# A decoder step's feed-forward part: up sums kept in PSUM, low parts shared anew between VectorE and GpSimd

## What is computed

```python
def merge_and_ffn(x, conv_out, attn_out, w_out, ffn_norm_g, w_gate, w_up, w_down):
    mix = jnp.concatenate([conv_out, attn_out.astype(conv_out.dtype)], axis=-1)
    x = x + jnp.einsum('bte,ed->btd', mix, w_out)
    h = rms_norm(x, ffn_norm_g)
    f = jax.nn.silu(jnp.einsum('btd,df->btf', h, w_gate)) * jnp.einsum('btd,df->btf', h, w_up)
    return x + jnp.einsum('btf,fd->btd', f, w_down)
```

## Time and profile before

| | us |
|---|---|
| median of 3 runs | 1693.53 |
| lowest and highest | 1683.49, 1693.72 |
| the profiled execution | 1688.96 |
| its span, first to last instruction | 1687.1 |
| TensorE busy in it | 1505.7 |
| VectorE busy | 1245.7 |
| GpSimd busy | 836.0 |
| ScalarE busy | 671.4 |

### The profile page before, as it was taken

One profiled execution on the slowest core, in us unless ns is written; L12 is line 12 of the kernel. 1 busy time (PEld: TensorE's weight loads), 2 busy tenths in 40 slices (PEclk: granted clock), 3 DMA queues, 4 the chain that ended last, 5 costly groups with the idle time before them and its releaser, 6 DMA issues.

```text
span 1687.1 us, 30660 instructions
## 1 busy us (share of the span) xinstructions
PE 1505.7 (89%) x10233; PEld 1371.8 (81%) x10233; DVE 1245.7 (74%) x2159; ACT 671.4 (40%) x1267; POOL 836.0 (50%) x643
## 2 busy tenths in 40 slices
PE   5999988889968878999889898999778999999889
PEld 4998767548756776999888888888778888988889
DVE  7799979999769844545867767666888666677775
ACT  4100268655356544522433333333243333333332
POOL 4544111211468400141766656666577666666664
PEclk9999989999969988999989999999889999999999
...
DMA packets 97160, 134.89 MB, mean 80 GB/s; under 512 B 15185, under 2 KB 51281, under 8 KB 96943
## 3 DMA queue, kind: packets, MB, share of 16 engines
...
## 4 chain that ended last, share of the span: by engine, by line
PE 50%; DVE 23%; issue 13%; ACT 7%; POOL 3%; DMA 2%; DVEq 1%; ACTq 0%; SPq 0%; POOLq 0%
PE ps L1162 14%; PE ps L1164 13%; PE ps L1163 13%; DVE raw_up L2987 2%; DVE mcnt L2578 2%; DVE ff L3043 2%; ACT f_hi L2231 2%; PE ps L1481 2%; PE ps L1469 1%; POOL w_lo L1093 1%; DVE x L3056 1%; DVE w_raw L2994 1%; ACT w_hi L2196 1%; DVE f_t L3031 1%; ACT rl L1904 1%
## 5 line engine op out<-in xcount | busy, mean ns | idle before, releaser
L1162 PE MATMUL ps<-hi_t,w_hi 128*128 128x272 f32 (+4 forms) x1672 | 498.2, 298 | 4.5 <-issue 2.5
L1164 PE MATMUL ps<-hi_t,w_lo 128*128 128x272 f32 (+4 forms) x1672 | 496.6, 297 | 0.0
L1163 PE MATMUL ps<-lo_t,w_hi 128*128 128x272 f32 (+4 forms) x1672 | 496.5, 297 | 0.0
L1162 PEld LDWEIGHTS ps<-hi_t,w_hi 128*128 128x128 f32 (+1 forms) x1672 | 315.8, 189 | 6.1 <-issue 4.1
L1163 PEld LDWEIGHTS ps<-lo_t,w_hi 128*128 128x128 f32 (+1 forms) x1672 | 315.7, 189 | 0.7
L1164 PEld LDWEIGHTS ps<-hi_t,w_lo 128*128 128x128 f32 (+1 forms) x1672 | 315.4, 189 | 0.6
L1162 PE MATMUL ps<-f_hi,w_hi 128*128 128x272 f32 x704 | 220.8, 314 | 83.5 <-DVE x L3056 66.5
L1093 POOL TENSOR_TENSOR w_lo<-w_raw,w_hi 128x512 fp32r<-128x512 f32 x132 | 185.1, 1402 | 133.0 <-ACT w_hi L2189 133.0
L1093 POOL TENSOR_TENSOR w_lo<-raw_up,w_hi 128x512 fp32r<-128x512 f32 x132 | 181.6, 1376 | 122.9 <-ACT w_hi L2189 122.9
L1162 PEld LDWEIGHTS ps<-f_hi,w_hi 128*128 128x128 f32 x704 | 140.2, 199 | 101.5 <-DVE x L3056 77.7
L1164 PE MATMUL ps<-f_hi,w_lo 128*128 128x272 f32 x704 | 211.3, 300 | 0.0
...
## 6 DMA issues: line engine op xcount, KB each, us to landing
raw_up<-in_w_up SPq DMA_DIRECT2D x88, 256.0 KB, 2.8
w_raw<-in_w_gate SPq DMA_DIRECT2D x88, 256.0 KB, 3.0
w_f<-in_w_down SPq DMA_DIRECT2D x88, 256.0 KB, 2.8
...
```

What stands on the lines that cost most here:

```text
L1162: pe.matmul(out, a_hi, b_hi, start=first, stop=False)
L1163: pe.matmul(out, a_hi, b_lo, start=False, stop=False)
L1164: return pe.matmul(out, a_lo, b_hi, start=False, stop=last)
```

## The change

- The sums of up (blocks 21, 11, 22 and 12) are written to the bank that the last of their products used, and stay there. `multiply` reads its up operand from the bank and writes the product into the same bank; `f_high` and `f_low` read it there. The tile `ff` is gone. TensorE's product 13 (step 6 of up), which writes the bank of block 21, now waits for that block's low part of f.
- The low parts of the down weights move from GpSimd to VectorE. Their high parts stand at the head of ScalarE's pair (two) and behind operand 10 (two); in pair 0 they stand later.
- GpSimd's low parts of gate and up operands are made as two instructions of 256 elements, its low parts of activations as four of 272.
- The sum `s1` gets a tile of its own. `make_s3` and `make_s2` of the next pair stand earlier among VectorE's sums, `add_down` 0 to 3 have no weight difference between them.
- In the opening, weight sums and activation sums stand at other outputs of the output projection; row scales of quarters 2 and 3 are made in pairs 8 and 9, and so is `normed` for them, which reads the scales from the bank (no copy by ScalarE).
- SyncE's loads follow: each half of the down weights is loaded behind VectorE's low parts, ahead of some parts of gate and up.

```diff
         def up_sum(part):
-            return {SUM21: ff[:, 1, 0:BLK], SUM11: p1_sum(1), SUM22: u3_sum(1), SUM12: u2_sum(1)}[part]
+            return ps[:, {SUM21: X_BANK, SUM11: Y_BANK, SUM22: Z_BANK, SUM12: X_BANK}[part][1], 0:BLK]
...
                 if not last:
                     for mat in range(2):
-                        sp.wait_ge(split_lo, n * PREP + (N_FFN + prepared(4 + mat)))
+                        sp.wait_ge(split_lo, n * NOPS + (N_FFN + 5 + mat))
                         load_part(mat, 2, after)
-                    for mat in range(2):
-                        sp.wait_ge(split_lo, n * PREP + (N_FFN + prepared(6 + mat)))
-                        load_part(mat, 3, after)
+                    sp.wait_ge(split_lo, n * NOPS + (N_FFN + 7))
+                    load_part(0, 3, after)
+                sp.wait_ge(dve_low, n * ND + KI_LOWS + 2)
+                load_down(row + P)
+                if not last:
+                    sp.wait_ge(split_lo, n * NOPS + (N_FFN + 8))
+                    load_part(1, 3, after)
                     for mat in range(2):
                         sp.wait_ge(s_done, n * 8 + (7 + mat))
                         load_part(mat, 0, after)
-                sp.wait_ge(split_lo, n * PREP + (N_FFN + down_prepared(1)))
-                load_down(row + P)
-                if not last:
+                    sp.wait_ge(dve_low, n * ND + KI_LOWS + ND)
+                    load_down(after)
                     for mat in range(2):
-                        sp.wait_ge(split_lo, n * PREP + (N_FFN + prepared(12 + mat)))
+                        sp.wait_ge(split_lo, n * NOPS + (N_FFN + 13 + mat))
                         load_part(mat, 1, after)
-                    sp.wait_ge(split_lo, n * PREP + (N_FFN + PREP))
-                    load_down(after)
...
             def operand_low(n, i, opening=False):
                 hi, lo = operand(i)
-                src, shaped = operand_source(i, opening)
-                pool.wait_ge(split_hi, n * PREP + (N_FFN + prepared(i)))
-                pool.tensor_tensor(shaped(lo), src, shaped(hi).bitcast(F32), ALU.subtract).then_inc(split_lo, 1)
-            def down_low(n, d):
-                hi, lo = down_operand(d)
-                pool.wait_ge(split_hi, n * PREP + (N_FFN + down_prepared(d)))
-                pool.tensor_tensor(lo, down_raw(d % 2), hi.bitcast(F32), ALU.subtract).then_inc(split_lo, 1)
+                src = operand_source(i)
+                pool.wait_ge(split_hi, n * HIGHS + (N_FFN + high_made(i, opening)))
+                for c in (slice(0, 256), slice(256, 512)):
+                    ins = pool.tensor_tensor(lo[:, c], src[:, c], hi[:, c].bitcast(F32), ALU.subtract)
+                ins.then_inc(split_lo, 1)
...
-                pool.tensor_tensor(lo, b_source(h, i), hi.bitcast(F32), ALU.subtract).then_inc(b_lo_pool, 1)
+                for k in range(4):
+                    ins = pool.tensor_tensor(lo[:, k, :], b_source(h, i)[:, k, :], hi[:, k, :].bitcast(F32), ALU.subtract)
+                ins.then_inc(b_lo_pool, 1)
...
             def weigh_pair(n, opening, switch, last):
-                for i in range(7, 12):
+                for i in range(7, NOPS):
                     operand_low(n, i, opening)
                     if opening and i == 9:
                         b_low(0, T1)
                 if opening:
+                    row_inverses(2)
                     row_inverses(3)
-                for d in range(2):
-                    down_low(n, d)
-                operand_low(n, 12, opening)
-                operand_low(n, 13, opening)
-                for d in range(2, ND):
-                    down_low(n, d)
                 if switch:
                     b_low(1, T3)
                 if last:
...
                 elif step == 5:
                     pe.wait_ge(comb, n * 14 + (3 + mat))
+                elif step == 6 and mat == 0:
+                    pe.wait_ge(comb, n * 14 + GATE_DONE[SUM21])
                 elif step == 6:
-                    pe.wait_ge(comb, n * 14 + (5 + mat))
+                    pe.wait_ge(f_lo_ready, n * 4 + SUM21)
...
-                pe.wait_ge(split_lo, n * PREP + (N_FFN + PREP))
+                pe.wait_ge(dve_low, n * ND + KI_LOWS + ND)
...
                     if opening and step == 0:
-                        row_scales(2)
-                    if opening and step == 2:
                         row_sums(3)
-                    if opening and step == 5:
-                        row_scales(3)
+                    if scaled is not None and step == 1:
+                        row_scales(scaled)
                 if opening:
-                    pe.wait_ge(rs_ready, NB + 4)
+                    pe.wait_ge(lnv_ready, NB + 4)
                     pe.wait_ge(x1_added, NOUT)
+                if scaled is not None:
+                    pe.wait_ge(xn_ready, 4 * NB + 8 + 2 * (scaled - 1))
                 down(n)
...
             def feed_pair(n, opening, switch, last):
+                if not opening:
+                    down_high(n, 0)
+                    down_high(n, 1)
                 take_p1(n, 0)
-                operand_high(n, 7, opening)
+                operand_high(n, 7)
                 take_p1(n, 1)
-                operand_high(n, 8, opening)
+                operand_high(n, 8)
                 if opening:
-                    take_scales(2)
                     b_high(0, T1)
                 if switch:
                     b_high(1, B11)
-                operand_high(n, 9, opening)
-                operand_high(n, 10, opening)
-                operand_high(n, 11, opening)
-                for d in range(2):
-                    down_high(n, d)
+                operand_high(n, 9)
+                operand_high(n, 10)
+                if opening:
+                    down_high(n, 0)
+                    down_high(n, 1)
+                else:
+                    down_high(n, 2)
+                    down_high(n, 3)
+                operand_high(n, 11)
                 if switch:
                     b_high(1, T3)
-                operand_high(n, 12, opening)
+                operand_high(n, 12)
                 silu(n, SUM21)
-                operand_high(n, 13, opening)
+                operand_high(n, 13)
                 f_high(n, SUM21)
                 if opening:
                     b_high(0, B22)
                 silu(n, SUM11)
-                for d in range(2, ND):
-                    down_high(n, d)
                 f_high(n, SUM11)
+                if opening:
+                    down_high(n, 2)
+                    down_high(n, 3)
+                if not last:
+                    operand_high(n + 1, 0)
                 if switch:
                     b_high(1, B21)
                 if not last:
-                    operand_high(n + 1, 0)
                     operand_high(n + 1, 1)
                 silu(n, SUM22)
                 f_high(n, SUM22)
-                if opening:
-                    take_scales(3)
                 if switch:
                     b_high(1, T1)
+                if not last:
+                    operand_high(n + 1, 2)
                 silu(n, SUM12)
                 if switch:
                     b_high(1, B22)
-                if not last:
-                    operand_high(n + 1, 2)
                 f_high(n, SUM12)
                 if not last:
                     operand_high(n + 1, 3)
...
                 c = tokens(h, j)
-                dve.wait_ge(rs_ready, NB + 2 * h + j + 1)
+                dve.wait_ge(lnb_mm, NB + 2 * h + j + 1)
                 for k in range(4):
                     kt = 4 * kh + k
                     ins = dve.scalar_tensor_tensor(ex[:, 2 * kh + j, k, :], x1[:, kt, c], kf[:, K_GF + kt:K_GF + kt + 1],
-                                                   rs_all[:, c], ALU.mult, ALU.mult)
+                                                   ps[:, SUMS_BANK, 0:BLK], ALU.mult, ALU.mult)
                 ins.then_inc(xn_ready, 1)
...
+            def down_low(n, d, opening=False):
+                hi, lo = down_operand(d)
+                dve.wait_ge(split_hi, n * HIGHS + (N_FFN + down_high_made(d, opening)))
+                dve.tensor_tensor(lo, down_raw(d % 2), hi.bitcast(F32), ALU.subtract).then_inc(dve_low, 1)
...
-                dve.tensor_tensor(p1_sum(mat), ps[:, Y_BANK[mat], 0:BLK], p1_sum(mat), ALU.add).then_inc(comb, 1)
+                dve.tensor_tensor((gate_sum, up_sum)[mat](SUM11), ps[:, Y_BANK[mat], 0:BLK], p1_sum(mat), ALU.add
+                                  ).then_inc(comb, 1)
...
             def multiply(n, part):
                 dve.wait_ge(glu_sig, n * 4 + (3 * CT + part))
                 dve.wait_ge(comb, n * 14 + UP_DONE[part])
-                dve.tensor_tensor(f_part(part)[2], up_sum(part), gate_sum(part), ALU.mult).then_inc(f_ready, 1)
+                dve.tensor_tensor(up_sum(part), up_sum(part), gate_sum(part), ALU.mult).then_inc(f_ready, 1)
             def f_low(n, part):
```

(59 more changed lines are left out.)

181 lines of the change are left out of this document (81 added, 100 removed).

## The result

Eight executions settle the time, four of each kernel on one chip: 1592.33 us median (1588.22 to 1598.26) after the change, 1693.62 (1683.49 to 1698.12) before. The ratio is 0.9412, with a 95% interval of 0.9359 to 0.9465. Forecast were 1581 us, 1562 to 1635. The profiled execution took 1588.22 us with a span of 1586.4, where the earlier trace rows come from one of 1687.1: 100.7 us less.

What follows compares the result with a forecast made beforehand. An order of waits, not a full engine, was taken as the bound. Savings of 71 (steady pairs), 16.6 (8, 9), 9 (10, 11) and 12.5 (opening), 109 us, put the span at 1578; forecast 1581 us, range 1562 to 1635.

Steps and rivals of the forecast that it cites:

- The bound and the steady pairs: Pairs 1 to 7 and 12 to 20: waits, not a full engine, bound them; 33.6 us each, 71 us saved.
- The stall of 0.4 us: Steady pair, fifth down output: TensorE due at 24.1 us waits 0.4 us for VectorE's first down addition.
- the stretch: VectorE's queue from the sum of product 8 to the first down addition: 13.8 us before, 11.7 forecast; decides the pair.
- Rival 1: Steady pairs: the stop moves but stays, 1 to 3 us a pair in place of 0.4; 1611 to 1641 us; chance 0.26.
- The bank writes, taken at nothing: VectorE writing to a bank, eight times a pair: no extra cost assumed; at worst 2.0 us a pair, 40 in all.
- Rival 2: Moving work between VectorE and GpSimd gives nothing: collisions cost 5.4 us a pair; time 1690; chance 0.05 together with rival 4.
- Rivals 3 and 4: 3: in-place bank instructions much dearer, about 1740 us, chance 0.05. 4: never-idle TensorE slows, no gain, 0.05 with rival 2.
- Pairs 8, 9 and 10: Normalizing split over pairs 8 and 9: 35.0 us each, 16.6 saved; pair 10, the switch: 42.5 for 47.87.
- Pair 11: Pair after the switch: 1.9 us over the new steady pair, 35.5 us for 39.22.
- no part is issued later: SyncE's queue: down loads move ahead only of weight parts that wait until 4.2 us or later by themselves.
- the wait for row sums 3: Opening: row sums 3, after step 0, wait about 2.5 us for the last squares, now behind `make_t4` on VectorE.
- The opening: Pair 0: three causes of stops leave, some 7 of 19.2 us excess remain; 52.45 becomes 40, saving 12.5 (6 to 16).

Runs made afterwards that it cites:

- both doubled runs: Changed kernel with VectorE making the two sums s1 twice: 1633.44 us; with its first two down low parts made twice at the pair's head: 1586.83 us.

## Why the prediction was right, and where it wasn't

**The bound and the steady pairs: right.** 33.6 us were forecast and 33.27 measured; 235.2 and 302.4 became 232.90 and 299.42. The stall of 0.4 us didn't come since the addition was 0.4 earlier (23.66 for 24.1), and both doubled runs show that the stretch was the right one. Rival 1, a stop that moves but stays, has no row in the steady pairs. **The bank writes, taken at nothing: right,** 0.43 to 0.45 us in every row, so the 40 us kept for them in the range weren't needed. The Trainium skill (Perfetto Trace Analysis, Optimizing Scalar/DVE Operations) states about 60 ns access time for VectorE on SBUF and 125 on PSUM; by it, as an estimate, the sum would have been 10 us higher. No row of this trace shows that difference: from the bank 272 elements take 424 ns into SBUF, and two operands in SBUF have a least of 427. **Rival 2, that moving work between the two engines gives nothing:** with the down low parts back on GpSimd a pair is 0.9 us longer, so the move gives. The same section of the Trainium skill says that the two share an SBUF read port, so that offloading between them might not help. The rows stretched here agree that they collide (1.21 us for 0.68, 1185 ns for 717); but in this kernel the move helped, by where the instructions stand. **Rivals 3 and 4** have no row for them either: nothing in place on a bank is above 450 ns, and the clock is 1.00 in all steady pairs.

**Pairs 8, 9 and 10: right.** 35.0, 35.0 and 42.5 forecast, 34.95, 34.92 and 42.64 measured. In pairs 8 and 9 the parts agree too (a stop of 0.83 us for about 1). In pair 10 some of the match is luck: 6.2 us of the 9.4 over a steady pair are stops, and 3.1 are TensorE busy for longer at a clock of 0.92, for which the prediction has no term.

**Pair 11: mis-sized.** 35.5 forecast, 38.07 measured: 1.2 us gained for 3.7. The term was the old pair's excess over pair 8 (1.4) carried over as 1.9, and it measured 4.8. The sentence that on SyncE's queue no part is issued later is wrong at this place and in the opening: up's last part is issued 8.1 us into pair 11 where it was 6.0, and 20.4 us into the opening where it was 13.5. I looked at what the down loads move past in a steady pair only. In pair 11 they compete with a store of 2176 KB (at most 1.4 us of stops), and the rest, by the timelines, is pair 10's work running over.

**The opening: the term that was mis-sized.** 12.5 us were forecast and 1.3 came (51.11 for 52.45). Each named cause did leave, and the wait for row sums 3 came as forecast (2.21 for about 2.5). The failed step is "GpSimd remains the last ahead of product 12 ... 0.5 to 2 us late": product 12 waits 3.37 us, and for VectorE's low part of B22; step 5 waits 3.48; and the down products wait 2.00 for the down low parts, now VectorE's. I costed what leaves and one engine of what stays. I didn't line up GpSimd's four-part low part of T1 (4.30 us), VectorE's two down low parts ahead of the second sum (2.07 us), and the transfer issued behind them (4.02 us of waiting). "Some 7 remain" has no room for the clock either: 6.8 us of the 17.8 over a steady pair come with it, beside 11.1 of stops. The runs that took two of these away gave 50.17 and 50.92 us, inside the spread of the unchanged opening; with the order of VectorE's queue changed too it took 46.85. As the stops read, several engines were late by similar amounts, so that taking one cause away brought out the next; what each is worth by itself is not shown. "An opening above 46 us" stood among the signs of a wrong step.

**The sum.** By the windows: steady pairs 76.4 us (71 forecast), pairs 8 and 9 16.7 (16.6), pairs 10 and 11 6.4 (9), opening 1.3 (12.5), together 100.8 of the span's 100.7 (pair 21 lost 0.1). The span was forecast at 1578 and measured 1586.4: the opening was 11.2 us and pairs 10 and 11 were 2.6 too favourable, and the steady pairs gave 5.4 more than forecast and hid that much of the miss. The other 3 us between 1581 and the median lie in the step from span to median. 109 off the median of 1693.53 would be 1584.5; the prediction took 1581, about 1 us above what its span of 1578 gives for the profiled execution (1579.9), and the measured median lies 4.1 above the profiled execution of 1588.22.
